# Expert rows of a PEER layer: U rows asked for 20 rows ahead of the V rows instead of 16

## What is computed

```python
for i in range(DEPTH):                                   # 2
    mix = hybrid_mixer(x, ...)
    x1 = layer_norm(DN_ALPHA * x + mix, ln1_g[i], ln1_b[i])
    y = peer(x1, peer_wq[i], peer_keys[i], peer_u[i], peer_v[i])
    e = sigmoid(x1 @ ple_wg[i] + ple_bg[i]) * (p[i] @ ple_wp[i])
    x = layer_norm(DN_ALPHA * x1 + y + e, ln2_g[i], ln2_b[i])

def peer(x, wq, sub_keys, expert_u, expert_v):           # 8 heads, 16384 experts
    ...                                                  # each token and head: ib, 16 experts; gb, their weights
    a = gelu(einsum('td,tkd->tk', xb, expert_u[ib]))
    return einsum('tk,tkd->td', a * gb, expert_v[ib])
```

## Time and profile before

| | |
|---|---|
| median of 3 runs | 3441.97 us (3438.99 to 3443.26) |
| span of the profiled execution | 3781.1 us |
| mean granted TensorE clock | 0.933 |
| pair loops in that span, first to last gather | 315 to 1877 us and 2197 to 3761 us |
| PE busy | 3004.2 us, 79% |
| DVE busy | 2120.8 us, 56% |
| POOL busy | 1984.4 us, 52% |
| ACT busy | 676.8 us, 18% |

### The profile page before, as it was taken

One profiled execution on the slowest core, in us unless ns is written; L12 is line 12 of the kernel. 1 busy time (PEld: TensorE's weight loads), 2 busy tenths in 40 slices (PEclk: granted clock), 3 DMA queues, 4 the chain that ended last, 5 costly groups with the idle time before them and its releaser, 6 DMA issues.

```text
span 3781.1 us, 25835 instructions
## 1 busy us (share of the span) xinstructions
PE 3004.2 (79%) x7696; PEld 1341.3 (35%) x7696; DVE 2120.8 (56%) x4948; ACT 676.8 (18%) x1658; POOL 1984.4 (52%) x2100
## 2 busy tenths in 40 slices
PE   8999777778778888777699987777777788887776
PEld 4555433333223323222245544333322233333222
DVE  1447665575555655665424476665656555656654
ACT  1331111111111112111013211111111111121110
POOL 0014455566665666666500145555566666666665
PEclk9999888889999999999999998888899999999999
DMA  4127899998999999999831278998899999989998
GB/s 153 67 70 256 313 342 344 346 350 338 399 368 351 355 384 355 348 371 367 336 129 67 70 269 316 353 347 339 335 363 407 363 352 363 385 329 362 371 370 321
DMA packets 360799, 1174.41 MB, mean 311 GB/s; under 512 B 36946, under 2 KB 75986, under 8 KB 360404
## 3 DMA queue, kind: packets, MB, share of 16 engines
q0 software_dynamic: 294912, 1073.87, 74.7%
q1 hardware_dynamic: 63284, 98.59, 7.6%
q10 hardware_dynamic: 2464, 0.31, 0.1%
HBM read 1170.54 MB, written 2.10 MB: 310 GB/s over the span
## 4 chain that ended last, share of the span: by engine, by line
PE 27%; DVE 18%; POOL 16%; issue 15%; another core or an unknown queue 11%; DMA 9%; ACT 4%; DVEq 1%; ACTq 0%; SPq 0%; POOLq 0%
DVE arena L1066 10%; POOL arena L567 9%; PE bank L1610 8%; POOL arena L558 8%; DMA arena<-in_peer_v,rows 5%; PE bank L1389 5%; DMA arena<-in_peer_u,rows 4%; PE yv L1389 3%; ACT arena L795 3%; PE bank L1416 2%; PE yv L1547 1%; PE bank L1437 1%; PE yv L1467 1%; PE bank L1547 1%
## 5 line engine op out<-in xcount | busy, mean ns | idle before, releaser
L1610 PE MATMUL bank<-arena 128*128 128x512 f32 x3840 | 1906.7, 637 | 523.0 <-DMA arena<-in_peer_v,rows 318.4
L1066 DVE CUSTOM_DVE_ANT_0 arena<-arena,xps 128x1024 f32<-128x1024 f32 x1024 | 1237.4, 1214 | 629.3 <-DMA arena<-in_peer_u,rows 464.2
L567 POOL DMA_INDIRECT arena<-in_peer_v,rows x1024 | 974.6, 952 | 714.1 <-issue 281.8
L1610 PEld LDWEIGHTS bank<-arena 128*128 128x128 f32 x3840 | 719.3, 200 | 1696.4 <-issue 938.4
L558 POOL DMA_INDIRECT arena<-in_peer_u,rows x1024 | 972.5, 950 | 552.1 <-issue 293.0
L607 ACT ACTIVATE arena<-arena 128x16 f32<-128x16 f32 x64 | 13.9, 218 | 1897.9 <-issue 1160.9
L795 ACT ACTIVATE arena<-keep,arena 128x128 f32<-128x128 f32 x960 | 294.2, 388 | 299.1 <-remote 147.8
L1416 PE MATMUL bank<-xT,arena 128*128 128x128 f32 (+1 forms) x1024 | 250.2, 399 | 57.4 <-issue 55.5
L1416 PEld LDWEIGHTS bank<-xT,arena 128*128 128x128 f32 x1024 | 165.3, 203 | 132.5 <-issue 72.3
L1389 PE MATMUL bank<-arena,xT 128*128 128x512 f32 (+1 forms) x448 | 187.1, 573 | 6.4 <-DMA arena<-in_w_in 4.3
L1389 PE MATMUL yv<-arena,xT 128*128 128x512 f32 (+1 forms) x320 | 132.6, 569 | 0.0
(11 more groups left out here) (288 smaller groups left out, 1966.1 us busy)
## 6 DMA issues: line engine op xcount, KB each, us to landing
arena<-in_peer_wq SPq DMA_DIRECT2D x32, 1024.0 KB
arena<-in_w_in SPq DMA_DIRECT2D x12, 2048.0 KB, 8.0
arena<-in_peer_u,rows POOLq DMA_INDIRECT x1024
arena<-in_peer_v,rows POOLq DMA_INDIRECT x1024
arena<-in_w_out SPq DMA_DIRECT2D x4, 2048.0 KB, 8.2
arena<-in_ple_wg SPq DMA_DIRECT2D x4, 2048.0 KB
arena<-in_mixer SPq DMA_DIRECT2D x2, 2112.0 KB, 19.4
ln<-in_ln SPq DMA_DIRECT2D x8, 512.0 KB, 7.9
```

Of the source, the lines that this page charges most:

```text
L567: e.indirect_dma_start(vrow[i % VR], None, a["peer_v"], bass.IndirectOffsetOnAxis(ap=rows[:, n % RR, k:k + 1], axis=0)).then_inc(v_in[i % ...
L1066: e.tensor_tensor_reduce(r, r, xps[:, :], 1.0, 0.0, ALU.mult, ALU.add, dots[:, n % 2, k:k + 1]).then_inc(u_free, 1)
L1610: ins = e.matmul(bank[m][:, :], diag[:, k, :], vrow[i % VR][:, m * 512:(m + 1) * 512], start=(h == 0 and k == 0), stop=(h == PH - 1 and k ...
```

## The change

`AHEAD = TOPK + 4` is new, and the loop over pairs becomes a loop over single rows: U row i + 20 is asked for ahead of V row i, where it was U row i + 16. The wait for the indices of a pair stands, as before, ahead of its first U row. Rings, semaphores and all other engines are the same.

```diff
+AHEAD = TOPK + 4
...
-                for n in range(1, PAIRS):
-                    if n + 1 < PAIRS:
-                        e.wait_ge(chosen_rows, n + 2)
-                    for k in range(TOPK):
-                        if n + 1 < PAIRS:
-                            gather_u(n + 1, k)
-                        gather_v(n, k)
+                def next_u(j):
+
+                    n, k = divmod(j, TOPK)
+                    if k == 0:
+                        e.wait_ge(chosen_rows, n + 1)
+                    gather_u(n, k)
+
+                for j in range(2 * TOPK, TOPK + AHEAD):
+                    next_u(j)
+                for i in range(TOPK, PAIRS * TOPK):
+                    if i + AHEAD < PAIRS * TOPK:
+                        next_u(i + AHEAD)
+                    gather_v(i // TOPK, i % TOPK)
```

## The result

| | before | after |
|---|---|---|
| median | 3441.65 us (3438.99 to 3443.26, 4 runs) | 3617.08 us (3608.4 to 3619.22, 4 runs) |
| ratio after to before | 1 | 1.0512, 95% interval 1.05 to 1.0524 |
| profiled span | 3781.1 us, and 3438.4 us (below) | 3617.1 us |

The change makes the kernel slower by 175 us, 5.1%. The forecast was 3618.

What follows compares the result with a forecast made beforehand. It took the waits at the head of POOL's single queue to bound the kernel. Per layer 68 + 6 + 10 + 0 + 6 + 3 - 5 = 88, for two layers 176: 3442 + 176 = 3618 us, range 3500 to 3690.

Steps and rivals of the forecast that it cites:

- Embedding pairs: Eight first dots per layer behind an embedding step, D(272) to D(320) and D(352) to D(400): 8.5 us each, 68 us.
- The way through POOL: Loop from D(384) through U(392), V(372) to V(383), embedding step, to D(400): 51.0 us, against a round of 48.5 seen.
- The 41.3 us at its shortest: The same loop through POOL in the kernel before, counting only what was taken as work after V(367).
- The choice of 8.5 us for a round: Loss per embedding round, taken near the upper end of a range from 2.5 to 9.7 to 9.9 us.
- Start and end: Per layer: V(24) starts later behind U(40), 6 us lost; the last U is out four V rows earlier, 5 gained.
- Block start at pair 8: U(136), waiting for D(128), stands ahead of V(116), so V(120) starts four steps later: 9.9 us, counted as 10 per layer.
- V rows that DVE adds: Rows 32 to 127, every fourth: 0 to 1 us for each of 24 rows, taken as 6 us per layer.
- The wait that was named as a sign of being wrong: V rows added by DVE waiting for DMA where they did not before.
- The count that left one microsecond: For V rows DVE adds: U(i+25) starts 22.3 us after U(i+16), needing D(i+17) at 21.2; 1 us left, now 11.
- Layer norms: Pairs 26 to 28, same loop without embedding step, some 8 us shorter: 0 to 2 us each, 3 per layer.
- Rival 4: Nothing: DMA engines limit throughout and hide POOL's waits; only the 10 us at the ends remain, 3432 us; chance 0.05.
- Rival 3: Faster: earlier U rows bring weights and P rows sooner in pairs 2 to 9, 3284 us; chance 0.05.

Runs made afterwards that it cites:

- distance 16: U row i + 16 ahead of V row i, the order of the kernel before, written with a distance and profiled again: 3439.11 us, profiled span 3438.4 us.
- The distance 20 in the late part alone: Against the kernel before: distance 16 up to V row 239, 20 from there on: 3604.31 us, ratio 1.0478.
- the distance 18: Against the kernel before: U rows 18 ahead of V rows throughout: 3505.06 us, ratio 1.0183.
- the sum moved by eight dots: The change with distance 20, but DVE adds each embedding eighth after the eighth dot of the next pair: 3492.96 us, ratio 1.0152 to the kernel before.
- the start alone: Against the kernel before: distance 20 up to V row 39 only, 16 from there on: 3439.89 us, ratio 1.0001.
- 6 alone: Block start alone, against the kernel before: distance 20 for V rows 96 to 135 only, 16 elsewhere: 3452.01 us, ratio 1.0039.
- the run with 20 up to row 239: Against the kernel before: distance 20 up to V row 239, 16 from there on: 3454.18 us, ratio 1.0042.

## Why the prediction was right, step by step

*What bounds.* Right in its main point: the order on POOL, not how early U rows come. The wait at the head of POOL's queue decides. The distance 20 cut DVE's wait for U by a third and made the kernel slower. One reading is a pair off: by the count of line 1091 the weights at 1497.56 are those of pair 23, not 22.

*Embedding pairs.* 68 us per layer forecast, 73.8 measured from pair 15 to pair 25. The way through POOL was given as 51.0 us, its part from V(367) to D(384) as 21.0; measured 51.1, 51.4 and 52.0 for the three full rounds from D(352) on, and 21.3. The 41.3 us at its shortest were 40.8 at distance 16. The choice of 8.5 us for a round lay a little low: the idle time in the earlier profile belonged to that execution, and seven of the eight pairs lose 9.2 to 11.3 us at PE, about the upper bound of 9.9. The eighth, pair 19, loses only 3.7: at distance 16 it takes 48.8 us already, and in it the second half of the embedding weights lands, 2.6 MB or 6.4 us at 409 GB/s (issued from 1201.1, landed at 1224.7). This fits a loss that is the loop's length less what the DMA engines need anyway, and no run tests it. The two misses, seven larger and one smaller, partly cancel. The distance 20 in the late part alone, the distance 18 and the sum moved by eight dots show the cause: the loss goes with the late part, grows by a step for each row, and leaves when DVE's first dots no longer stand behind the sum, but for the one round that ACT's copy holds.

*Start and end.* +6 and -5 forecast, +5.3 and -4.2 measured. The sizes are right and the description is not, so the match at the start is partly luck: the wait of 13.79 us at U(40) from which the 6 was read the earlier trace rows belonged to that one execution, and at distance 16 and after U(40) starts after 0.30 us of idle time, as every gather does that waits for nothing. What remains is the four U rows more ahead of V(16). They are lent, and paid back where the distance ends, as the start alone shows; in the change that is the end of the layer.

*Block start at pair 8.* 10 us forecast, 6.8 measured in after (5.2 to 12.0) and 6 alone. U(136) waits 13.2 us there in the run with 20 up to row 239, for D(128), which waits 11.9 us for ACT's copy. At distance 16 it waits 6.6 us (12.05 in the earlier profile). The wait grows by 6.6 us, as much as PE loses, and not by the four steps of 9.9. The mechanism is right, the size too high.

*V rows that DVE adds.* 6 us forecast, 0 measured: pairs 2 to 6 lose nothing beyond the loan. The wait that was named as a sign of being wrong is there, 136.7 us after against 0.5 at distance 16, and costs nothing; that PE is the later one in these pairs explains it and was not tested by itself. So the sign told nothing. The count that left one microsecond was close: two rows further it binds.

*Layer norms.* 3 us forecast, 9.6 measured from pair 25 to pair 29. What was too small is the 0 to 2 us allowed for each of three pairs: pairs 26 to 28 lose 3.2, 2.4 and 2.8 us at PE and pair 29 another 1.3. The rounds from D(432) and D(448) are 43.1 and 45.3 us after, against 40.0 and 42.9: 6 to 8 us below 51, as forecast or a little longer.

*The sum.* 88 per layer forecast; measured 90.3 in layer 0 by the table, and 87.7 as half of 175.4. Block start and DVE's rows too high by 9 and layer norms and embedding pairs too low by 12 nearly cancel; that the sum came within 1 us of 3617 is luck, and it is better than its terms.

*Rivals.* Rival 4's premise is true of the kernel before: its DMA engines are full, and what looked like slack in the earlier trace rows belonged to that one execution. The conclusion is not: the order of the queue emptied them, 403 to 343 GB/s. The rule that was weighed beside it, the Trainium skill, page "DMA: Bandwidth & Descriptors", section "Where 436 GB/s comes from", puts HBM's limit at about 358 GB/s per core. The trace does not agree for these gathers on one core: at distance 16 the slices of the pair loops stand at 394 to 409 GB/s, and the measurement decides. Rival 3 needed P to wait for weights; DVE did get its U rows earlier and P did not gain.

## What to carry to other kernels

In a queue that serves two rings in order, the prefetch distance minus the ring's depth says which consumer stands at the head; a larger distance makes the other stream wait for a later consumer, and where a dependence leads back from that stream to the consumer, every row of distance is paid in every round once that loop is longer than what the other limits need (here from 16 on; going from 16 to 12 gained nothing in the rounds). A bandwidth that is full tells that there is nothing to gain by asking earlier, and not that there is nothing to lose. Before costing a loop from idle time that no row explains, get a second profile: a span far above the median is the sign.

## What the runs showed of the hardware that was not expected

One profiled execution took 3781.1 us, and the same order of gathers profiled again 3438.4, with 3439 to 3442 for the timed runs: a single profile can hold a tenth of the time that no other run shows, spread over waits that look like the kernel's own. No run shows where that time came from.

Gathers of 512 KB keep one core's DMA engines at 394 to 409 GB/s over more than a thousand microseconds of a layer. The median from issue to landing (the profile page's last part: transfer, issuing queue, operation and count, median us) is longer in the faster kernel; that a gather then waits behind others in full DMA engines is a reading of this and not shown. At distance 16:

```profile
arena<-in_peer_u,rows POOLq DMA_INDIRECT x1024, 10.5
arena<-in_peer_v,rows POOLq DMA_INDIRECT x1024, 10.6
```

and after:

```profile
arena<-in_peer_u,rows POOLq DMA_INDIRECT x1024, 8.0
arena<-in_peer_v,rows POOLq DMA_INDIRECT x1024, 8.2
```
